# Two transformer blocks on one core: the mixer's thin sums placed elsewhere, and the ends of the first nets' up slots ordered anew

## What is computed

```python
for l in range(DEPTH):                       # first block, DEPTH = 2
    z = rms_norm(h_res, attn_norm_g[l]) @ w_in[l]
    c_q, c_kv, k_pe, rq, rk, rv, rg = split(z)
    ...
    q = rms_norm(q, q_g); k = rms_norm(k, k_g)   # over the 192 of each head: the query and key sums
    ...
    o = silu(rg) * o                             # retention gate: four tiles of 128 columns
    h_res = h_res + concat(y_mla, y_ret) @ w_out[l]
    hf = rms_norm(h_res, ffn_norm_g[l])
    gate, up = split(hf @ w_gate_up[l])          # 2 x 2816 columns
    h_res = h_res + (silu(gate) * up) @ w_down[l]
```

## Time and profile before

| | |
|---|---|
| median of 3 runs | 2304.03 us (2303.01 to 2305.49) |
| profiled execution | 2302.83 us, of which its span is 2301.2 us |
| PE busy | 2258.3 us, 98% of the span |
| DVE busy | 1462.8 us, 64% |
| ACT busy | 847.0 us, 37% |
| POOL busy | 160.2 us, 7% |
| chain that ended last | PE 79%, issue 11%, DVE 6%, ACT 3%, DMA 1% |

### The profile page before, as it was taken

How to read it: one execution, slowest core, us unless ns; L and a number is a source line. 1 busy time by engine, 2 the same in 40 slices (tenths; PEclk the granted TensorE clock), 3 DMA queues, 4 the chain that set the end, 5 groups by cost and what they waited for, 6 DMA issues and landing times.

```text
span 2301.2 us, 37388 instructions
## 1 busy us (share of the span) xinstructions
PE 2258.3 (98%) x14172; PEld 2033.1 (88%) x14172; DVE 1462.8 (64%) x2310; ACT 847.0 (37%) x1130; POOL 160.2 (7%) x235
## 2 busy tenths in 40 slices
PE   8999999999999999999999999999999999999998
PEld 8999999999999988888888888888888888879998
DVE  4547777556778787678778767773333346556555
ACT  4445444435634432222432222232212234445443
POOL 0110000130000110001001101000000001000000
PEclk9999999999999999999999999999999999999999
DMA  6225665323665565455335545433233223123553
GB/s 230 98 74 195 206 239 174 124 83 103 210 237 187 180 207 183 164 192 177 106 130 204 182 162 199 160 115 110 77 105 109 71 95 127 56 74 128 173 192 128
DMA packets 65483, 343.21 MB, mean 149 GB/s; under 512 B 7152, under 2 KB 10480, under 8 KB 42608
## 3 DMA queue, kind: packets, MB, share of 16 engines
q1 hardware_dynamic: 44656, 266.47, 33.3%
q0 software_dynamic: 20736, 75.51, 9.8%
HBM read 340.90 MB, written 1.05 MB: 149 GB/s over the span
## 4 chain that ended last, share of the span: by engine, by line
PE 79%; issue 11%; DVE 6%; ACT 3%; DMA 1%; POOL 0%; DVEq 0%; SPq 0%; ACTq 0%; POOLq 0%
PE gpt L841 20%; PE gpt L843 19%; PE gpt L842 19%; DVE w_lo L1951 2%; ACT w_hi L1461 2%; PE gpt L938 1%; PE gpt L766 1%; PE gpt L939 1%; PE gpt L940 1%; PE gpt L767 1%; PE gpt L768 1%; PE mbt L1121 1%; PE gpt L1336 1%; PE gpt L1337 1%; PE gpt L1338 1%
## 5 line engine op out<-in xcount | busy, mean ns | idle before, releaser
L841 PE MATMUL gpt<-xn_hi,w_hi 128*128 128x512 f32 (+2 forms) x2256 | 747.3, 331 | 5.7 <-DVE w_lo L1951 5.7
L842 PE MATMUL gpt<-xn_lo,w_hi 128*128 128x512 f32 (+2 forms) x2256 | 742.8, 329 | 0.0
L843 PE MATMUL gpt<-xn_hi,w_lo 128*128 128x512 f32 (+2 forms) x2256 | 742.7, 329 | 0.0
L1951 DVE TENSOR_TENSOR w_lo<-raw,w_hi 128x2048 fp32r<-128x2048 f32 (+2 forms) x280 | 567.6, 2027 | 249.7 <-ACT w_hi L1461 249.5
L1461 ACT ACTIVATE w_hi<-raw 128x2048 fp32r<-128x2048 f32 (+2 forms) x280 | 476.4, 1702 | 390.9 <-PE gpt L843 356.5
L841 PEld LDWEIGHTS gpt<-xn_hi,w_hi 128*128 128x128 f32 x2256 | 426.5, 189 | 46.6 <-issue 7.1
L842 PEld LDWEIGHTS gpt<-xn_lo,w_hi 128*128 128x128 f32 x2256 | 426.6, 189 | 37.6
L843 PEld LDWEIGHTS gpt<-xn_hi,w_lo 128*128 128x128 f32 x2256 | 426.5, 189 | 37.5
L841 PE MATMUL gpt<-mid_hi,w_hi 128*128 128x512 f32 (+2 forms) x996 | 333.1, 334 | 4.7 <-DVE mid_lo L2149 4.5
L842 PE MATMUL gpt<-mid_lo,w_hi 128*128 128x512 f32 (+2 forms) x996 | 332.2, 334 | 0.0
L843 PE MATMUL gpt<-mid_hi,w_lo 128*128 128x512 f32 (+2 forms) x996 | 332.2, 334 | 0.0
(11 more groups left out here) (341 smaller groups left out, 2734.5 us busy)
## 6 DMA issues: line engine op xcount, KB each, us to landing
raw<-in_up_a SPq DMA_DIRECT2D x72, 1024.0 KB, 4.7
ada_w<-in_ada POOLq DMA_DIRECT2D x144, 512.0 KB, 3.5
raw<-in_up_b SPq DMA_DIRECT2D x60, 1024.0 KB, 4.8
raw<-in_down_a SPq DMA_DIRECT2D x48, 768.0 KB, 4.3
raw<-in_down_b SPq DMA_DIRECT2D x48, 640.0 KB, 3.9
raw<-in_win SPq DMA_DIRECT2D x16, 1024.0 KB, 4.8
raw<-in_qkv SPq DMA_DIRECT2D x12, 1024.0 KB, 4.8
raw<-in_wout SPq DMA_DIRECT2D x8, 1024.0 KB, 4.8
```

Source lines behind the costliest of these rows:

```text
L841: mm(o, w_hi[b][:, j, :], hi(k), start=(k == 0), stop=False)
L842: mm(o, w_hi[b][:, j, :], lo(k), start=False, stop=False)
L843: last = mm(o, w_lo[b][:, j, :], hi(k), start=False, stop=(k == kt - 1))
L1951: V.tensor_tensor(w_lo[b][:, 0:tiles, :], raw[b][:, 0:tiles, :], w_hi[b][:, 0:tiles, :].bitcast(F32), ALU.subtract).then_inc(lo_ready, 1)
```

## The change

Three edits (the hunks stand in the order mixer, ACT, DVE). In the mixer, `q_thin` spreads its twelve sums over all eight steps of gate 0 (by turns one and two to a step) where they had the first four; the key sums and their wait move from gate 0's second half to gate 1's first half. On ACT, in the two nets of the first block, the loop over up slots is written out. In these nets the last pair of up slots is ordered anew: DVE does the last slot's product and low part ahead of its weight split, ACT does silu and rounding ahead of the split, and DVE's modulation and context-norm work of both slots comes after all of it.

```diff
@@ -1009,7 +1009,7 @@
 
                 def q_thin(k):
 
-                    for i in range(3 * k, 3 * k + 3):
+                    for i in range(3 * k // 2, 3 * (k + 1) // 2):
                         q, h = i // HEADS, i % HEADS
                         if q not in m_tiles(L):
                             continue
@@ -1020,7 +1020,7 @@
 
                 def k_thin(k):
 
-                    for i in range(3 * k - 12, 3 * k - 9):
+                    for i in range(3 * k, 3 * k + 3) if k < KT // 2 else ():
                         t0 = TT1[i // HEADS][0]
                         last = mm(mb[0][:, i:i + 1], ksq[:, i % HEADS, t0:t0 + P], ones[:, 0:1], start=True, stop=True)
                         if i == 11:
@@ -1067,14 +1067,14 @@
                 pe.wait_ge(qk_sq, L * 19 + 11)
                 gate(0, first, q_thin)
                 r_pv(3)
-                pe.wait_ge(qk_sq, L * 19 + 19)
-                gate(0, second, k_thin)
+                gate(0, second, q_thin)
 
                 wait_evac(pe, L, T_KV + 7)
                 pe.wait_ge(rp_ready, L * HEADS + 4)
                 pe.wait_ge(q_mean, L + 1)
                 v_turn(1)
-                gate(1, range(KT))
+                pe.wait_ge(qk_sq, L * 19 + 19)
+                gate(1, range(KT), k_thin)
 
                 pe.wait_ge(k_rcol, L + 1)
                 pe.wait_ge(v_ready, L * 6 + 6)
@@ -1561,23 +1561,29 @@
                         else:
                             act.wait_ge(mid_f, j0 + j + 1)
                         A(mid_hi[:, j, 0:n], midf[:, b, 0:n], ACT.Copy).then_inc(mid_h, 1)
-                    with act.Fori(0, up - 1) as i:
-                        for b in range(2):
-                            if late is None:
+                    if late is None:
+                        with act.Fori(0, up - 1) as i:
+                            for b in range(2):
                                 silu(p0 + i, i * 2 + b, b)
-                            split(p0 + i + 1, b, SIDE_T)
-                            if late is not None:
+                                split(p0 + i + 1, b, SIDE_T)
+                                round_hidden(p0 + i, i * 2 + b, b)
+                    else:
+                        for i in range(up - 1):
+                            for b in range(2):
+                                split(p0 + i + 1, b, SIDE_T)
                                 silu(p0 + i, i * 2 + b, b)
-                            round_hidden(p0 + i, i * 2 + b, b)
+                                round_hidden(p0 + i, i * 2 + b, b)
                     for b in range(2):
+                        if late is not None and b == 0:
+                            split(p0 + up, b, cnt)
+                        silu(p0 + up - 1, 2 * up - 2 + b, b)
                         if late is None:
-                            silu(p0 + up - 1, 2 * up - 2 + b, b)
-                        split(p0 + up, b, cnt)
-                        if late is not None:
-                            silu(p0 + up - 1, 2 * up - 2 + b, b)
+                            split(p0 + up, b, cnt)
                         round_hidden(p0 + up - 1, 2 * up - 2 + b, b)
-                        if half == 1 and ni == CTX_NORM:
-                            norm2_half(ni, *HALF_MOD[ni], 1, (b,))
+                        if late is not None and b == 1:
+                            split(p0 + up, b, cnt)
+                    if half == 1 and ni == CTX_NORM:
+                        norm2_half(ni, *HALF_MOD[ni], 1, (0, 1))
                     p0 = p0 + up
                     if half == 1 and ni == CTX_NORM:
                         for i in range(KT // 2 - 1):
@@ -2175,17 +2181,22 @@
                             hidden(p0 + up - 1, 2 * up - 2 + b, b)
                             split(p0 + up, b, cnt)
                             hidden_lo(2 * up - 2 + b, b)
-                        else:
-                            scaled_slot(up - 1, b, cnt)
-                            if b == 1:
-                                hidden_lo(2 * up - 1, 1)
-                        if half == 1 and ni == CTX_NORM:
-                            if b == 0:
-                                dve.wait_ge(cs_row, 1)
-                                derive(0, 0)
-                            scaled_half(ni, 1, b)
-                            lo_half(ni, 1, b)
-                        modulation(2 * half, up - 1, b)
+                            modulation(2 * half, up - 1, b)
+                    if scaled_by is not None:
+                        scaled_slot(up - 1, 0, cnt)
+                        hidden_scaled(p0 + up - 1, 2 * up - 1, 1)
+                        hidden_lo(2 * up - 2, 0)
+                        hidden_product(p0 + up - 1, 2 * up - 1, 1)
+                        hidden_lo(2 * up - 1, 1)
+                        split(p0 + up, 1, cnt)
+                        for b in range(2):
+                            if half == 1 and ni == CTX_NORM:
+                                if b == 0:
+                                    dve.wait_ge(cs_row, 1)
+                                    derive(0, 0)
+                                scaled_half(ni, 1, b)
+                                lo_half(ni, 1, b)
+                            modulation(2 * half, up - 1, b)
                     p0 = p0 + up
                     if half == 1:
                         clear_sum(ni)
```

## The result

The changed kernel took 2319.59 us (median of 10 runs, 2308.90 to 2332.94) against 2303.14 us (10 runs, 2297.76 to 2305.49). The ratio is 1.0075, with a 95% interval of 1.0059 to 1.0092: slower by 16.5 us, where I forecast 4.7 us less. The spread has grown from 8 to 24 us. Its profiled execution took 2317.19 us.

A forecast was written before the change was run, and what follows sets the result against it. PE, busy 98% of the span, loses time only where it waits or runs at half clock. Mixer 6.6 + table loads 4.8 - last pair 5.05 - clock 1.6 = 4.75 us gained: 2304.03 to 2299.3 us, range 2293.0 to 2304.0.

The forecast's parts named there:

- Clock in gates 0 and 1: Mixer: full clock from gate 0 through gate 1 in both layers; all of the mixer's 6.6 us gain comes from clock.
- The rival by the rule on transposes: Gate 1: transposes don't count as busy PE, so key sums lose the clock in both layers; 2303.5 us (0.06).
- The wait for `q_mean`: Mixer, after gate 0: PE idles some 0.35 us for DVE's query mean, which had half a gate as cover.
- The wait for `k_rcol`: Mixer, before the `k_row` matmuls: PE waits 1.1 us for POOL's power, taken as 114.69 to 116.96.
- The step that failed first: Mixer: the two new waits cost 2.9 us of what the clock gives, leaving 6.6 us gained.
- the 4.4 us wait in the feed-forward net: Layer 1's second half, down slot 2: clock price between nothing and 3.2 us, taken as 1.6 us lost.
- The slower rival: Gate 1 to gate 2's retention sums: key sums bring a 13.7 us low stretch in both layers; 2309.9 us (0.07).
- a wait of 2.02 us: End of a feed-forward half, PE waiting for the last `mid_lo`: one of 2.02 us left the clock at full.
- Table loads: Layer 1's net, first half: nine of ten ACT table loads go, ten up slots 62.49 to 57.69, 4.8 us gained.
- The last pair, second halves: Layer 1: 3.3 us lost, waits of 1.2 and 4.4 us replacing 2.2; layer 0: 0.75 us lost.
- The last pair, first halves: Feed-forward nets' first halves: no norm work and longer slots, so about 0.5 us lost each.
- The third low stretch: Layer 0's attention, around 155 to 162 us: rival that it does not come, worth 3.2 us, 2296.1 us (0.15).

The follow-up runs named there:

- e10: Kernel before plus ACT's slots written out and the mixer edit with gate 2's first half over the wait, old last pair: 2296.23 us, ratio 0.9969.
- e11: Kernel before with only the key sums moved and gate 2's first half over the wait, query sums left in place: 2301.58 us, ratio 0.9991.
- e1: Kernel before plus the mixer edit alone: 2310.83 us, ratio 1.0037.
- e5: Kernel before with only the key sums moved into gate 1, query sums left in gate 0's first half: 2309.96 us, ratio 1.0036.
- e7: As e6, with the key sums also spread over all eight steps of gate 1: 2316.47 us, ratio 1.0059.
- e6: Kernel before plus the mixer edit, with gate 2's first half ahead of the row matmuls, over the wait for POOL's power: 2298.76 us, ratio 0.9987.
- e9: Kernel before plus the mixer edit, with DVE's gate 2 split held back until POOL's power is done: 2300.83 us, ratio 0.9988.
- e12: As e10, with the new last-pair order but DVE's and ACT's postponed work of b = 0 at its old place: 2298.55 us, ratio 0.9979.
- e2: Kernel before plus ACT's up-slot loop written out alone, old last pair: 2298.47 us, ratio 0.9976.
- e3: Kernel before plus the new order of the last pair alone, ACT's loop kept as a hardware loop: 2314.80 us, ratio 1.0049.

## Why the prediction was wrong

**What bounds the kernel** was read rightly: time is lost where PE waits or runs at 1.2 GHz.

**Clock in gates 0 and 1: right.** It stayed at 2.4 GHz up to the `k_row` matmuls in both layers of the changed kernel and of the mixer edit alone. The rival by the rule on transposes did not show there. Gate 1 isn't safe, though: one layer of e10 and one of e11 fell at the end of its three-sum steps (486.45 and 112.17 us), for 3.41 us each, and no run tells whether the transposes ahead of the sums had a part in it.

**The wait for `q_mean`:** forecast 0.35, measured 0.41 and 0.35 us. **The wait for `k_rcol`:** forecast 1.1, measured 1.91 in both layers. I took POOL's power at the 2.27 us of the earlier trace rows, though the edit changes which engine starts first, DVE's split or POOL. To the first `k_row` matmul the gain was 3.4 and 0.6 us, not 4.8 and 1.8. Of the 1.4 and 1.2 us that are missing, the longer wait is 0.8 each.

**The step that failed first** is the sentence that the new waits "cost 2.9 us of what the clock gives". They cost the clock itself: of the mixer edit's loss about half is waits (4.2 us) and half clock (4.5 us), where I had 9.5 us of clock gained. I asked whether the sums in gate 1 would bring it down and gave a clock price only to the 4.4 us wait in the feed-forward net. The wait for POOL, between dense sums and row matmuls, got only its own length. The slower rival named this place, "gate 1 to the retention sums of gate 2", but as a matter of the sums, with 0.07. The runs show +7 us for the mixer edit against the forecast -6.6, between -3 and -5 us once the wait is covered or shortened to 1.0 us, and +13 us when the sums are thinned but another wait of 1.48 us comes in. So in gate 1 it is above all the wait behind the sums that decides. Dense sums can lose the clock without a wait, as in the kernel before, where PE never stood in those 20.14 us. In my profiles with a wait of 1.5 us or more there, five of eight layers have a low stretch behind or in it (the changed kernel, e1, e5, e7); in those with 1.0 us or none (e6, e9, e10, e11, e12) none of ten has one that begins behind the first `k_row` matmul and ahead of the attention, and two have the one of 3.4 us in gate 1 told of above. What sets the odds in one execution stays open.

One premise was read off a single execution: that a wait of 2.02 us "left the clock at full". Nine profiles have this wait unchanged (before, e1, e2, e5, e6, e7, e9, e10, e11). In five of them a low stretch of 3.41 us begins within 1.2 us of its end, as here in e10, where the first matmul behind it already takes 0.58 us instead of 0.39:

```profile
732.21 0.58 PE L841 MATMUL gpt<-mid_hi,w_hi 128*128 128x256 f32 x1 [2.02 <-DVE mid_lo L2154]
```

**Table loads: right.** Forecast 4.8, measured 4.55 us in the trace and 5.6 us as an edit alone.

**The last pair, second halves: right.** Layer 1: waits forecast 1.2 and 4.4, measured 1.38 and 4.19 us, and 1.6 us for the clock behind them against 3.41 us at 1.2 GHz, 1.7 us. Layer 0: 0.75 against 1.1 us. (The replay takes DVE on from 734.75, though its split ends at 734.83; that is 0.1 us and changes nothing.)

**The last pair, first halves: the second failed step,** "about 0.5 us each". They cost 4.5 us in layer 0, a low stretch of 3.41 us among them, and 3.4 us in layer 1. I moved `ada` and counted its 2.48 us on DVE, but not the DMA that it releases: the next modulation stands in down slot 1 or 2, and its weights now come too late.

**The third low stretch** came as before (158.85 to 165.68 us), so that rival gave nothing.

**How much each miss weighs**, in the profiled execution, whose span grew by 14.3 us where I forecast 4.75 less: the mixers +4.7 against -6.6, so 11.3 us; the first halves' ends +7.9 against +1.0, so 6.9 us; the second halves' ends +6.3 against +5.65, and the up slots -4.55 against -4.8, together 0.8 us. That is the whole 19 us. How it splits differs from execution to execution, as the clock does.

**The range** left out 2319 because the only slower case was priced by one fall per layer, and because the first halves had no slower case at all. A change that brings new waits at so many places of a PE-bound kernel has many places to lose the clock.

## What to carry to other kernels

In a kernel bound by PE, price a new wait of PE by what the clock may do behind it as well as by its length: here 0.9 us of wait in two places was worth 10 us. Don't take a wait for harmless because one profile kept its clock there: the one of 2.02 us did in four profiles and not in five. Look for cover before moving work; half a gate laid over the wait turned +7 us into -5 us. When a step is postponed, follow the buffers that it frees and the DMA that waits for them to the next step that needs them, and when an edit changes which of DVE and POOL starts first, don't take POOL's time from the old trace.

## What the hardware showed unexpectedly

- The same program falls to 1.2 GHz at different places in different executions: the unchanged mixer needed 20.14 us in layer 0 of the kernel before and 13.78 us in e3. One profile doesn't show the usual case; the mean clock of all runs does.
- POOL's power of 128x12 took 2.27 us when it started 0.05 us ahead of DVE's subtraction of 128x1024 float32 and 3.18 us when it started 0.16 us behind. The Trainium skill says in SBUF — State Buffer, section "🔬 SBUF: two separate sides", that DVE and GpSimd share a port pair, and that, when a DVE operation has two SBUF inputs (as this subtraction) and a GpSimd one reads SBUF, the one that starts first holds the pair for its whole instruction while the other is blocked. The second case agrees (DVE's remaining time was 1.06 us, POOL lost 0.91). The first agrees only in half: POOL kept its time, but DVE, which came second, was not blocked and took its usual 1.23 us.
- ACT's table loads of 1.28 us in a loop were real time: with nine of the ten gone PE gained 4.55 us, though ACT was busy only 37% of the span.
